# Weighing the expert rows when they leave PSUM, and adding them to the residual by DMA

## The reference, cut to what matters

```python
def hier_moe(h, router_group, router_expert, w_gate, w_up, w_down):
    ...
    gate = g_gate * jax.nn.softmax(e_val, axis=-1)      # two gates for each token
    ...
    def expert_block(args):
        toks, e = args
        xb = x_pad[toks]
        hb = jax.nn.silu(xb @ w_gate[e]) * (xb @ w_up[e])
        return hb @ w_down[e]
    ...
    y = jax.ops.segment_sum(y_blocks.reshape(P, D).astype(f32) * slot_w[:, None], slot_tok, num_segments=T + 1)[:T]

def reference(...):
    for layer in range(DEPTH):
        ...                                             # a mixer: h = h + mix
        h = h + hier_moe(rms_norm(h, norm_ffn_g[layer]), ...)
```

## Time and profile before

| | us |
|---|---|
| median of 3 runs (1571.92 to 1575.39) | 1574.41 |
| the profiled execution | 1577.22 |
| its span in the profile | 1575.2 |
| TensorE busy in the span | 1524.2 (97%) |
| VectorE (DVE) busy | 592.8 (38%) |
| ScalarE (ACT) busy | 351.7 (22%) |
| GpSimd (POOL) busy | 272.3 (17%) |

### The profile page before, as it was taken

One profiled execution on the slowest core, in us unless ns is written; L12 is line 12 of the kernel. 1 busy time (PEld: TensorE's weight loads), 2 busy tenths in 40 slices (PEclk: granted clock), 3 DMA queues, 4 the chain that ended last, 5 costly groups with the idle time before them and its releaser, 6 DMA issues. The chain is left out here.

```text
span 1575.2 us, 27527 instructions
## 1 busy us (share of the span) xinstructions
PE 1524.2 (97%) x11800; PEld 824.4 (52%) x11800; DVE 592.8 (38%) x1313; ACT 351.7 (22%) x581; POOL 272.3 (17%) x296
## 2 busy tenths in 40 slices
PE   7999999999999999999999999999999999999996
PEld 4887545544444444435566666645544444444442
DVE  5737634332322222225354444435332232222225
ACT  3152611100000000013445554431010000000003
POOL 9542000000000000000344444420000000000000
PEclk9999999999999999999999999999999999999999
DMA  6733086999999999995511121115999999999996
GB/s 222 270 85 120 14 345 254 398 420 428 427 426 427 426 426 428 427 419 245 214 55 55 67 89 62 55 76 211 399 414 426 426 426 427 427 427 428 426 423 252
DMA packets 63613, 472.24 MB, mean 300 GB/s; under 512 B 13041, under 2 KB 21241, under 8 KB 35584
## 3 DMA queue, kind: packets, MB, share of 16 engines
q1 hardware_dynamic: 58544, 462.52, 71.4%
q0 software_dynamic: 4800, 7.87, 1.3%
q10 hardware_dynamic: 144, 0.05, 0.0%
HBM read 452.03 MB, written 24.27 MB: 302 GB/s over the span
## 5 line engine op out<-in xcount | busy, mean ns | idle before, releaser
L930 PE MATMUL ps<-sb_ring,sb_work 128*56 128x512 f32 x2048 | 453.4, 595 | 17.6 <-issue 14.9
L930 PEld LDWEIGHTS ps<-sb_ring,sb_work 128*56 128x56 f32 x2048 | 146.6, 130 | 311.2 <-issue 311.0
L945 PE MATMUL ps<-sb_ring,sb_work 128*56 128x512 f32 x1024 | 230.8, 593 | 0.6 <-DMA sb_ring<-in_w_down_dram 0.6
L1653 POOL DMA_INDIRECT expert_rows<-sb_work,sb_ri x60 | 54.7, 912 | 998.6 <-DVE sb_work L2133 714.5
L713 PE MATMUL ps<-sb_work,sb_h 128*64 128x112 f32 x4096 | 222.4, 262 | 0.0
L713 PEld LDWEIGHTS ps<-sb_work,sb_h 128*64 128x64 f32 x4096 | 204.1, 137 | 34.8 <-issue 30.8
L2124 DVE TENSOR_TENSOR sb_work<-sb_work,ps 56x512 f32<-56x512 f32 x64 | 70.2, 1098 | 319.9 <-ACT sb_work L1451 319.8
L1180 PE MATMUL ps<-sb_work,sb_ring 128*128 128x512 f32 x384 | 170.4, 598 | 0.0
L1451 ACT ACTIVATE sb_work<-ps 56x512 f32<-56x512 f32 x64 | 37.6, 588 | 434.0 <-PE ps L930 434.0
L945 PEld LDWEIGHTS ps<-sb_ring,sb_work 128*56 128x56 f32 x1024 | 67.1, 130 | 113.5 <-issue 112.1
L1466 ACT ACTIVATE sb_work<-ps 56x512 f32<-56x512 f32 x60 | 35.4, 590 | 394.6 <-PE ps L945 355.6
(11 more groups left out here) (255 smaller groups left out, 1348.6 us busy)
## 6 DMA issues: line engine op xcount, KB each, us to landing
sb_ring<-in_w_down_dram SPq DMA_DIRECT2D x62, 2048.0 KB, 25.3
sb_ring<-in_w_gate_dram SPq DMA_DIRECT2D x54, 2048.0 KB, 23.0
sb_ring<-in_w_up_dram SPq DMA_DIRECT2D x54, 2048.0 KB, 27.0
sb_ring<-in_w_gate_dram SPq DMA_DIRECT2D x18, 1024.0 KB, 10.5
sb_ring<-in_w_up_dram SPq DMA_DIRECT2D x18, 1024.0 KB, 12.8
sb_ring<-in_c_w_in_dram SPq DMA_DIRECT2D x8, 2048.0 KB, 8.4
sb_ring<-in_ab_w_in_dram SPq DMA_DIRECT2D x8, 1024.0 KB, 8.4
expert_rows<-sb_work SPq DMA_DIRECT2D x2, 4096.0 KB, 21.4
```

The lines of the kernel that those rows point to most:

```text
L930: mm = nc.tensor.matmul(dst[64 * z:64 * z + CAP, :], me["xgT"][:, j, c, q * CAP:(q + 1) * CAP], wblock(slots[z], NC)[:, c, :], start=(c == ...
L945: mm = nc.tensor.matmul(dst[64 * z:64 * z + CAP, :], src[:, c * CAP:(c + 1) * CAP], wblock(slots[2], FC)[:, c, z * 512:(z + 1) * 512], sta ...
L1653: return g.indirect_dma_start(out=y_d[l], out_offset=bass.IndirectOffsetOnAxis(ap=idx, axis=0), in_=me["rows"][0:CAP, j, :], in_offset=Non ...
```

## The change

Each expert's rows are multiplied by their gates before they are scattered, the scatter is otherwise the same plain write, and GpSimd adds the rows from HBM into `h` in SBUF by eight transfers with an add, two waves of four.

- `slot_table` multiplies two more products, so that the gate of every slot of every expert lies in PSUM on both halves of the partitions; DVE copies it to `slot_gate`. DVE forms the matrix `G` for it in `slot_lists`.
- The gates must be there earlier: the Exp moves to the end of the mixer, before the activation table for Silu is loaded, `gate_values` to before expert 0.
- From expert 2 on the two evictions multiply by `slot_gate`; experts 0 and 1, evicted before the table is there, are multiplied by GpSimd in SBUF, each before its scatter.
- `rows_back`, `combine`, `add_rows` and the diagonal matrices go. GpSimd issues the eight adding transfers behind its last scatter's landing; each of the second wave waits for the first of its tile. `add_late` of a tile waits for both (`h_back`).
- SP loads the first `c_w_in` as soon as slot 0 is free, the second when all adding transfers have landed.

```diff
-                    sp.dma_start(yrow(t), back[t]).then_inc(yrow_in[t], 16)
...
             for i, (s, _) in enumerate(w1_in):
+                if i == 0:
+                    wait_full(sp, ("gu", 0, NS + 1))
                 if i == 1:
-                    sp.wait_ge(h_ready, 4)
+                    sp.wait_ge(h_back[NT - 1], 32)
...
+                for i in range(2 * NT):
+                    for z in range(2):
+                        mm = nc.tensor.matmul(dst[64 * z:64 * z + CAP, NE:2 * NE], me["A"][:, i // NT, i % NT, :],
+                                              me["G"][:, i // NT, i % NT, :], start=(i == 0), stop=(i == 2 * NT - 1))
...
                 copy_raw(l, NT - 1)
+                act.wait_ge(route_in, l + 1)
+                A(ex, ex, ACT.Exp).then_inc(route_exp, 1)
                 A(warm[:], eps_t[:], ACT.Silu).then_inc(act_step, 1)
...
                 A(half_row(me["rows"][0:CAP, e % 2, :], 0), chunked(bank(("dn", l, e))[0:CAP, :]), ACT.Copy,
+                  scale=me["slot_gate"][0:CAP, e:e + 1] if e >= 2 else 1.0).then_inc(half_out, 1)
...
                 for e in range(NK):
                     wait_drained(pool, ("dn", l, e))
+                    if e < 2:
+                        own = me["rows"][0:CAP, e, :]
+                        g.tensor_scalar(own, own, me["slot_gate"][0:CAP, e:e + 1], None, ALU.mult).then_inc(weighed, 1)
+                        pool.wait_ge(weighed, 2 * l + e + 1)
                     scatter_rows(l, e % 2, ri[:, e:e + 1]).then_inc(scattered[e % 2], 16)
...
                 pool.sem_inc(ov_done, 1)
+                for b in range(PB):
+                    wait_full(pool, ("pick", l, NK // PICK, b))
+                for k in range(2):
+                    for t in range(NT):
+                        if k == 1:
+                            pool.wait_ge(h_back[t], 16 * (2 * l + 1))
+                        g.dma_start(out=h[:, t, :], in_=y_d[l][k * T + t * P:k * T + (t + 1) * P, :], accum_op=ALU.add
+                                    ).then_inc(h_back[t], 16)
...
             def add_late(l, t):
+                dve.wait_ge(h_back[t], 32 * (l + 1))
...
-                combine(l, 0)
-                combine(l, 1)
                 if l == 0:
                     add_late(l, 0)
                     add_late(l, 1)
                     norm_col(2, 0)
                     norm_rows(2, 0)
-                    combine(l, 2, (1,))
+                    add_late(l, 2)
                     norm_col(2, 1)
                     norm_rows(2, 1)
-                    add_late(l, 2)
                     add_late(l, 3)
```

More of the change, by code:

```diff
@@ L304, in trunk @@
         scattered = [sem(f"scattered{j}") for j in range(2)]
-        yrow_in = [sem(f"yrow_in{t}") for t in range(NT)]
         rsum_ready, act_step = sem("rsum_ready"), sem("act_step")
@@ L1095, in late_add @@
                     dst = opens(job)
-                    mm = nc.tensor.matmul(dst[:], late_pick[:, t * P:(t + 1) * P],
-                                          me["rows"][:, 1, nb * 512:(nb + 1) * 512], start=True, stop=(t < NT - 2))
-                    if t < NT - 2:
-                        fills(mm, job)
-            def add_rows(l, t, ks):
-                pe.wait_ge(late_ready, 2 * l + 2)
-                pe.wait_ge(yrow_in[t], 16 * (l + 1))
-                for nb in range(2):
-                    for k in ks:
-                        mm = nc.tensor.matmul(bank(("add", l, t, nb))[:], diag[:, k if t == NT - 1 else 2, :],
-                                              yrow(t)[:, k, nb * 512:(nb + 1) * 512], start=False, stop=(k == ks[-1]))
-                    fills(mm, ("add", l, t, nb))
+                    fills(nc.tensor.matmul(dst[:], late_pick[:, t * P:(t + 1) * P],
+                                           me["rows"][:, 1, nb * 512:(nb + 1) * 512], start=True, stop=True), job)
             def more_blocks(l):
@@ L1148, in moe @@
                 last_experts(l)
-                for t in range(NT - 1):
+                for t in range(NT):
                     late_add(l, t)
-                add_rows(l, NT - 2, (0,))
-                late_add(l, NT - 1)
-                if l == 0:
-                    turn_rows(2, (0,))
-                add_rows(l, NT - 1, (0, 1))
             moe(0)
@@ L1508, in moe @@
                     act_expert(l, e)
-                    if e == 2:
-                        act.wait_ge(route_in, l + 1)
-                        A(ex, ex, ACT.Exp).then_inc(route_exp, 1)
                 last_experts(l)
@@ L2104, in row_table @@
                 v.tensor_scalar(flag[:, l:l + 1], top[:, 5, 0:1], CAP + 0.5, None, ALU.is_gt).then_inc(flag_ready, 1)
+                for z in range(2):
+                    part = slice(64 * z, 64 * z + CAP)
+                    v.tensor_copy(me["slot_gate"][part, :], bank(job)[part, NE:2 * NE])
                 drains(v.tensor_copy(tab[:, 0, :], bank(job)[0:CAP, 0:NE]), job)
@@ L2132, in out_rows @@
                     dve.wait_ge(scattered[e % 2], 16 * (l * (NK // 2) + e // 2))
[L2133 to L2134 removed]
+                own, src = half_row(me["rows"][0:CAP, e % 2, :], 1), chunked(bank(("dn", l, e))[64:64 + CAP, :])
+                if e == 2:
+                    dve.wait_ge(table_ready, l + 1)
+                if e >= 2:
+                    drains(v.tensor_scalar(own, src, me["slot_gate"][64:64 + CAP, e:e + 1], None, ALU.mult), ("dn", l, e))
+                else:
+                    drains(v.tensor_copy(own, src), ("dn", l, e))
             def hidden(l, e):
@@ L2159, in dve_expert @@
                     slot_lists(l)
-                if e == 3:
-                    gate_values(l)
                 if e == 4:
@@ L2316, in moe @@
                 selections(l, 1)
+                gate_values(l)
                 for e in range(NS):
```

78 lines of the change are left out of this document (36 added, 42 removed).

## The result

The changed kernel takes 1585.85 us (median of 4 runs, 1582.68 to 1587.36); the kernel before, run on the same chip, 1574.66 (4 runs, 1571.92 to 1575.39). The ratio is 1.0072 with a 95% interval of 1.0052 to 1.0092: slower by 11.2 us. 1586.0 was predicted.

A forecast was written before the change was run, and what follows sets the result against it. Bound: the DMA stream of weights in the expert stages, DVE's chain at layer 1's end. Layer 0's 1.5 + 6.0 and layer 1's 1.5 + 2.5 gave +11.5 us on the 1574.41 median: 1586 us, range 1568 to 1596.

The forecast's parts named there:

- The adding packet: Layer ends: each packet of the eight adding transfers costs two plain ones, 19.1 us in all; chance 0.47.
- Layer 0: End of layer 0: last addition done at 736.5 instead of 730.5 us, +6.0 us, passed on whole to layer 1.
- The first `c_w_in` load: End of layer 0: this load now stands in front of the adding transfers and delays their landing by 4.9 us.
- Layer 1: End of layer 1: last landing at 1569.1 us, where the last addition had begun at 1566.59, so +2.5 us.
- The last weights: Layer ends: adding packets delay the last expert's weights by 3.9 us if doubled, hidden under the wait for the transfers.
- The bound of 13 small packets: Layer ends: at most 13 adding packets per engine get between the weight packets, 1.9 us plain or 3.9 doubled.
- The beginning: Start of each layer's expert stage: later scatters let 1.5 us pass into the DMA stream; bounds 0 and 2.7 us.
- that of `slot_table` and what followed from it: Beginning of the expert stage: 16 more small matmuls take 2.0 us, and two copies of 0.17 us delay the row table.
- the case that the prediction had named at 1.0 and not taken: In `slot_table`: the added matmuls cost 1.0 us instead of 2.0 if the two halves run side by side.
- The first scatter: Beginning of the expert stage: its issue moves from 299.1 to about 304.5 us, its landing from 308.1 to 313.5.
- TensorE behind it: Beginning of the expert stage: TensorE is 2.7 us late afterwards in layer 0, about 2.0 in layer 1.
- The sign that the prediction gave for it: Before L936 of expert 3: TensorE's gap grown by 2 to 3 us, and a DMA share below 0.9 there.

The follow-up runs named there:

- cw_behind: Changed kernel, with layer 0's first `c_w_in` load held until all adding transfers have landed: 1586.39 us, ratio 1.0078 to the kernel before.
- first_adds: Changed kernel, with the first wave's four transfers adding and the second wave's four as plain writes: 1579.16 us, ratio 1.0032 to the kernel before.
- plain_write: Changed kernel, with all eight transfers as plain writes into `h` instead of adds: 1571.66 us, ratio 0.9988 to the kernel before.
- tile_order: Changed kernel, with both rows of tiles 0 and 1 transferred first, then those of tiles 2 and 3: 1587.14 us, ratio 1.0088 to the kernel before.
- weights_first: Changed kernel, with GpSimd holding the adding transfers until expert 31's last weights have landed: 1590.65 us, ratio 1.0097 to the kernel before.
- read_back: Changed kernel with the old ends: SP reads weighed rows back plainly, DVE and TensorE add them: 1575.86 us, ratio 1.0010 to the kernel before.

## Why the prediction was right

- **The adding packet, the choice that decided.** Twice a plain one was taken, 19.1 us for eight. The landings come 2.47 us apart, 19.8 for eight, and the engine time of a packet is 0.334 us, where two plain packets of the earlier trace rows make 0.30. The prediction divided by all 427 packets; by the 395 of 4 KB a plain one is 0.161, two are 0.32, and the eight 20.6 us. That the factor is two was a reading of the nearest row, given a chance of 0.47; no row had shown it. The rule of the Trainium skill ("Collectives: The Full Stack", section "The bandwidth ceiling: the fold count and why AG ≠ RS ≠ AR") gave a factor of 1.93. Against the plain packet on the same queue the runs give 1.83, and 1.98 by the landings (2.47 against 1.25 us), so they agree with it.
- **Layer 0.** Last landing predicted 36.6 us after the start, measured 35.2 and 36.4, in the profiled execution and the second one; the end later by 6.0 predicted, by 5.5 and 6.8 measured. The step held. The first `c_w_in` load in front of the landings is a real term (cw_behind lands 4.2 us earlier than the first profile of the change, 5.3 than the second; 4.9 predicted), though moving the load behind them saved nothing.
- **Layer 1.** +2.5 predicted, +2.0 and +4.3 measured. The last addition was predicted right behind the last landing; in both profiles DVE waits for the landings of tiles 0 and 1, and the last tiles follow at DVE's own pace with norms and `weigh` between. The landing of the first tiles is what makes this end late. The number held, the path to it is another than the sum's, and first_adds shows the same (first addition at 22.0 us instead of 17.2, end 3.6 us longer than plain_write's).
- **The last weights.** 3.9 us late "under the wait" was the prediction. Against the two profiles of before they are late by 2.0 to 2.2 us in layer 0 and 2.9 to 4.1 in layer 1 in the first profile of the change, by 5.1 to 5.3 and 3.7 to 5.0 in the second. The bound of 13 small packets between was thus too low in one execution. "Under the wait" was right: in every kernel with adding transfers in its first wave a landing releases the first addition after the copy, except in layer 1 of tile_order, where TensorE does; and weights_first, where the weights are not late, is no faster.
- **The beginning was mis-sized.** 1.5 us for each layer were predicted, 3.0 in all; the three stretches give 0.9 and 2.1, with the first stage, in which a part of layer 0's beginning lies, -1.7 and +1.6, and read_back 1.5 (0 to 3). The step that failed is that of `slot_table` and what followed from it: the row table comes 0.8 us later (3.23 after the first product, 2.44 before), not 2.3, since the added products of the two halves run side by side, the case that the prediction had named at 1.0 and not taken. The first scatter was 3.75 us late instead of 5.4, and TensorE behind it by -0.25 us in the first pair, +1.7 in the second, instead of 2.7. The cover behind `slot_table`, up to 2 us of variation in a scatter's own landing, is of the size of the effect, so one execution couldn't have told it. The sign that the prediction gave for it, TensorE's gap before L936 of expert 3 grown by 2 to 3 us, did not show (0 and 0.85 us, 1.09 and 0 before), and the DMA share fell below 0.9 in one profile only (0.83 between 305 and 310 us).
- **What cancels.** The ends were put at 8.5 us and measured 7.5 and 11.1 in the two pairs; all that stands before them at 3.0 and measured -1.7 and +1.6. The spans of the pairs lie 5.8 and 12.7 us apart, the medians 11.2. So the total of 11.5 agrees with the medians' 11.2 to a few tenths partly by luck: the ends were by the second pair too low, the beginnings by both too high. How the 11.2 is shared between the two ends can't be said better than by the two pairs.
- **What did not fail.** The Exp and its table loads, `gate_values`, `G` and the product inside the evictions were put at nothing: they lie inside read_back's 0 to 3 us. They were not tried one by one.

## What to carry over

An addition in a DMA is not free because it removes an instruction: price it at two packets, and ask which landing the next engine waits for: here it was the last tile's in layer 0 and the first tiles' in layer 1. At both ends the DMA engines were full while the additions ran. The combines of both layers, 13.1 us of DVE, went, and the ends still grew by 7.5 to 11 us, since the additions in DMA cost 13 us more than plain transfers would. When a sum is to be taken off DVE's chain, look at the other compute engines first, and check that they don't slow each other down.

## What the hardware showed unexpectedly

- An adding transfer of 128 x 1024 f32 from HBM into SBUF costs 0.334 us of engine time per 4 KB packet, a plain write on the same queue 0.183; the landings come 2.47 and 1.25 us apart (the latter in one interval of plain_write, 1548.07 to 1549.32). Alone in the queue an adding packet costs the same 0.337 us. Its issue takes GpSimd 0.86 us instead of 0.53.
- 0.183 on GpSimd's queue is more than the 0.161 of a plain 4 KB packet on SP's (from the earlier trace rows; the page's rounding allows 0.17 to 0.20); why was not tried.
- Products into the two halves of TensorE's columns ran side by side: 30 in 0.96 us, the time of 15 in one half alone.
- Two additions of 128 x 1024 from SBUF on DVE took 3.25 us each instead of 1.23 while GpSimd did the same kind, itself at 2.49 and 3.33 us instead of 2.36; beside DVE's additions from PSUM GpSimd kept its 2.36.
- TensorE's granted clock fell to 0.64 of 2.4 GHz between 730 and 740 us, after it had waited 7.11 us for DVE; 32 products then took 3.67 us instead of 1.97, while the stretch from the last addition to the mixer grew by 0.3 to 0.5 us.
